# Stick-breaking attention with the keys on the partitions and its running sums on TensorE

## What is computed

```python
z = einsum('bqhd,bkhd->bhqk', qi, k) * scale            # scale = 0.125
strict = kpos[None, :] < qpos[:, None]
log_beta = log_sigmoid(z)
log_one_minus = where(strict, log_sigmoid(-z), 0.0)
after = lax.cumsum(log_one_minus, axis=3, reverse=True) - log_one_minus
weights = exp(where(strict, log_beta + after, -inf))
out = einsum('bhqk,bkhd->bqhd', weights, v)
```

## Time and profile before

| | us |
|---|---|
| median of 3 runs | 4967.44 (4967.3 to 4972.65) |
| the profiled execution | 4978.45 |
| its span in the trace | 4976.6 |
| stick stage of the first such block, 3214.2 to 3371.2 | 157.0 |
| stick stage of the second, 4313.2 to 4471.9 | 158.7 |

### The profile page before, as it was taken

The page is one execution under the profiler, slowest core; times in us unless marked ns, Lnnn a source line. Parts: engine busy times, 40 slices in busy tenths (PEclk is TensorE's granted clock), DMA queues, the critical chain, the costliest instruction groups (busy, mean ns, idle before and its releaser), DMA issues. The chain is left out here.

```text
span 4976.6 us, 90377 instructions
## 1 busy us (share of the span) xinstructions
PE 4460.7 (90%) x38676; PEld 3119.2 (63%) x38676; DVE 2113.1 (42%) x3803; ACT 1495.0 (30%) x2632; POOL 792.0 (16%) x499
## 2 busy tenths in 40 slices
PE   6899899988998899979999798978999988878999
PEld 3566666666555554465443776757788866656787
DVE  2555554554355552131111446354443446345343
ACT  2343333332222221010000334453232334443232
POOL 0021111110132230000000221243000321333000
PEclk9899999988999999989999899989999999999999
DMA  6200000000110123427999311214222211214221
GB/s 228 71 28 11 17 19 17 5 24 16 43 43 29 48 87 131 154 107 302 405 403 411 122 63 50 69 49 168 88 98 77 94 56 48 69 61 154 98 102 51
DMA packets 86824, 512.05 MB, mean 103 GB/s; under 512 B 10504, under 2 KB 11032, under 8 KB 45848
## 3 DMA queue, kind: packets, MB, share of 16 engines
q1 hardware_dynamic: 86424, 506.28, 26.9%
HBM read 476.85 MB, written 29.38 MB: 102 GB/s over the span
## 5 line engine op out<-in xcount | busy, mean ns | idle before, releaser
L229 PE MATMUL ps<-rounded,rounded 128*128 128x512 f32 (+2 forms) x7968 | 1660.4, 367 | 44.3 <-DVE rounded L240 23.7
L229 PEld LDWEIGHTS ps<-rounded,rounded 128*128 128x128 f32 x7968 | 1338.1, 193 | 302.8 <-issue 36.1
L229 PE MATMUL ps<-lower 128*128 128x512 f32 (+10 forms) x4976 | 1075.0, 393 | 56.3 <-issue 22.8
L229 PE MATMUL ps<-upper 64*64 64x64 f32 (+8 forms) x15584 | 834.2, 259 | 152.0 <-DVE upper L268 38.2
L291 ACT ACTIVATE upper<-ps 128x512 f32<-128x512 f32 (+6 forms) x953 | 440.2, 491 | 1671.0 <-PE ps L229 1230.6
L229 PEld LDWEIGHTS ps<-upper 64*64 64x64 f32 (+4 forms) x15584 | 595.7, 145 | 419.8 <-issue 190.6
L229 PEld LDWEIGHTS ps<-lower 128*128 128x128 f32 (+3 forms) x4976 | 576.7, 184 | 442.9 <-issue 376.6
L229 PE MATMUL ps<-lower,upper 64*64 64x64 f32 (+6 forms) x7248 | 607.6, 305 | 47.5 <-DMA lower<-in_ada 20.3
L2620 POOL TENSOR_TENSOR rounded<-lower,rounded 128x1024 fp32r<-128x1024 f32 (+2 forms) x90 | 273.1, 3035 | 1952.3 <-ACT rounded L291 1952.0
L291 ACT ACTIVATE upper<-upper 128x512 f32<-128x512 f32 (+9 forms) x693 | 341.1, 500 | 584.1 <-DVE upper L248 131.4
L229 PEld LDWEIGHTS ps<-lower,upper 64*64 64x64 f32 (+3 forms) x7248 | 334.6, 143 | 258.7 <-issue 198.8
(11 more groups left out here) (91 smaller groups left out, 2351.0 us busy)
## 6 DMA issues: line engine op xcount, KB each, us to landing
lower<-in_ew SPq DMA_DIRECT2D x140, 1024.0 KB, 10.4
upper<-in_ew SPq DMA_DIRECT2D x52, 1024.0 KB, 13.1
lower<-in_b0f SPq DMA_DIRECT2D x16, 2048.0 KB, 7.4
lower<-in_b1f SPq DMA_DIRECT2D x16, 2048.0 KB, 7.7
upper<-in_ada SPq DMA_DIRECT2D x18, 1024.0 KB, 5.3
lower<-in_wrkv SPq DMA_DIRECT2D x8, 1728.0 KB, 7.3
lower<-in_b0g SPq DMA_DIRECT2D x24, 512.0 KB, 3.8
gad<-upper SPq DMA_DIRECT2D x48, 256.0 KB, 3.8
```

Source lines behind the costliest of these rows:

```text
L229: return self.e.matmul(out, lhsT, rhs, start=start, stop=stop)
```

## The change

The scores are computed transposed, with the keys on the partitions: for head `hh` and key block `j`, `ck` is the stationary side and the queries 128*j to 511 are the moving side. A head's lower triangle of blocks takes 1280 columns of PSUM in place of four units. The mask of the diagonal blocks is added by a matmul of the identity with a 128 x 128 mask (fp32r). The scale of 0.125 moves into the copy of the queries (`c0`). The running sum over keys, which was a scan of VectorE along the free side, becomes matmuls along the partitions, with a triangle of -1 and a full square of -1 as weights, on two fp32r parts (`lost` and `rest`) of the losses; they are written over the scores in the same PSUM banks, and VectorE adds the copy of the scores (`chance`) to them. The weights then already have the form that the value matmuls want, and the transposes and their copies go. Every elementwise step handles a whole head (128 x 1280). Two heads are in flight, each with three PSUM banks of its own (`take_at`).

The order of the stage is written out: scores of head `hh`; sums of head `hh-1`; `early` filler items; values of head `hh-1`; `late` filler items. The remainders of the weights (`part`) that stand behind `meet B` are computed by VectorE. The diff, cut to its core:

```diff
-    p2 = {"mla": add(k <= q), "sb": add(k < q), "g2": add((k <= q) & ((q - k) % 4 == 0)),
+    p2 = {"mla": add(k <= q), "sb": add(i[:, None] < i[None]), "tri": -f(i[:, None] >= i[None]), "one": -f(up | True), "g2": add((k <= q) & ((q - k) % 4 == 0)),
...
-    b.on = RC[:, 2048:2560]
-    b.trip = [RA[:, 1536 * z:1536 * z + 1536] for z in range(6)]
+    at = ROUNDED + 4096
+    b.soft = [k.plain(at + 3840 * z, 1280) for z in range(2)]
+    b.chance = [k.plain(47272 + 1280 * z, 1280) for z in range(2)]
+    b.lost = [k.rounded(at + 3840 * z + 1280, 1280) for z in range(2)]
+    b.raw = [k.plain(at + 3840 * z + 2560, 1280) for z in range(2)]
+    b.rest = [k.rounded(at + 3840 * z + 2560, 1280) for z in range(2)]
+    b.sums = k.rounded(43176, 512)
...
+    end = b.order.index(("meet", "B"))
+    for key in (step[1] for step in b.order[end:] if step[0] == "part"):
+        b.units[key].late = True
...
+def part_done(k, l, key):
+    return k.parts.dve if k.b2[l].units[key].late else k.parts.pool
+
+
+def part_vector(k, v, l, key):
+    u = k.b2[l].units[key]
+    if u.late:
+        v.wait_ge(k.parts.act, "high", l, key)
+        v.tt(k.parts.dve, u.low, u.raw, u.high.bitcast(F32), SUB, "low", l, key)
+
+
 def part_gpsimd(k, g, l, key):
     u = k.b2[l].units[key]
+    if u.late:
+        return
...
-    drain([lane("stick", 32, 5, z) for z in range(6)], filler, 1.4)
+    for hh, (early, late) in enumerate(((2, 2), *[(3, 3)] * 6, (3, 2), (3, 0))):
+        if hh < 8:
+            out.append(("stick", hh, 0))
+        if hh:
+            out.append(("stick", hh - 1, 1))
+        out += itertools.islice(filler, early)
+        if hh:
+            out.append(("stick", hh - 1, 2))
+        out += itertools.islice(filler, late)
...
+BLOCK_AT = (0, 512, 1024, 896)
+
+
+def block_cut(j, i=None):
+
+    at = BLOCK_AT[j] + 128 * ((i or j) - j)
+    return slice(at, BLOCK_AT[j] + 512 - 128 * j)
...
-            pe.wait_ge(k.parts.pool, "low", l, key)
+            pe.wait_ge(part_done(k, l, key), "low", l, key)
...
+    def stick(hh, s):
+        team, slot, use = k.lane[hh % 2], hh % 2, ("stick", l, hh)
+        e = slice(64 * slot, 64 * slot + 64)
+        if s == 0:
+            ps = banks.take_at(use, 3 * slot, 3)
+            pe.wait_ge(M.act, "sums", l)
+            for j in (0, 1, 3, 2):
+                pe.mm(ps[:, block_cut(j)], b.ck[e, hh // 2, 128 * j:128 * j + 128], b.cq[e, hh // 2, 128 * j:512], j != 3, False)
+                last = pe.mm(ps[:, BLOCK_AT[j]:BLOCK_AT[j] + 128], b.sums[:, 256:384], b.sums[:, 384:512], False, j != 1)
+            last.then_inc(team.pe.up("score", l, hh), 1)
+            return
+        ps = k.pair(use)
+        if s == 1:
+            pe.wait_ge(team.dve, "parts", l, hh)
+            pe.wait_ge(team.act, "kept", l, hh)
+            for j in (3, 2, 1, 0):
+                for i in range(j, 4):
+                    for part in (b.lost[slot], b.rest[slot]):
+                        last = pe.mm(ps[:, block_cut(j, i)], b.sums[:, 128:256] if i > j else b.sums[:, 0:128],
+                                     part[:, block_cut(i)], j != 1 and i == j and part is b.lost[slot],
+                                     j != 3 and i == 3 and part is b.rest[slot])
+            last.then_inc(team.pe.up("less", l, hh), 1)
+        else:
+            pe.wait_ge(team.act, "exp", l, hh)
+            for i in range(4):
+                for j in range(i + 1):
+                    p = b.chance[slot][:, BLOCK_AT[j] + 128 * (i - j):BLOCK_AT[j] + 128 * (i - j) + 128]
+                    for half in (slice(0, 64), slice(64, 128)):
+                        last = pe.mm(ps[half, 1280 + 64 * i:1344 + 64 * i], p[:, half], b.cv[:, j, 64 * hh:64 * hh + 64],
+                                     j == 0, j == i)
+            last.then_inc(team.pe.up("value", l, hh), 1)
+            banks.give(use, team.dve, "value", l, hh)
...
-            v.copy(P.dve, dst, v3(ps, 256)[:, :, 0:tok_width(t)] if name == "tok" else ps, *use)
+            if t == "c0":
+                v.ts(P.dve, dst, ps, 0.125, MUL, event=use)
+            else:
+                v.copy(P.dve, dst, v3(ps, 256)[:, :, 0:tok_width(t)] if name == "tok" else ps, *use)
...
-    def stick(u, s):
-        o = Unit(k, l, "stick", u)
-        t, nk = o.lane.dve, o.nk
-        z, a_, r = (o.buf[:, 512 * q:512 * q + nk] for q in range(3))
-        if s == 1:
-            v.wait_ge(o.lane.pe, "score", *o.u)
-            v.stt(t, z, k.pair(("score", *o.u))[:, 0:nk], 0.125, o.mask, MUL, ADD, "score", *o.u)
-        elif s == 2:
-            v.wait_ge(o.lane.act, "log", *o.u)
-            v.stt(t, a_, z, 0.0, a_, MAX, ADD)
-            v.wait_ge(t)
-            v.e.tensor_tensor_scan(r[:, ::-1], b.on[:, 0:nk], a_[:, ::-1], 0.0, MUL, ADD).then_inc(t.up("sum", *o.u), 1)
-        elif s == 3 and o.i % 2:
-            v.wait_ge(o.lane.pe, "turn", *o.u)
-            v.copy(t, z, k.pair(("turn", *o.u))[:, 0:nk], "turn", *o.u)
-        elif s == 4:
-            v.wait_ge(o.lane.pe, "value", *o.u)
-            v.copy(t, o.out, k.pair(("value", *o.u))[:, 0:64], "value", *o.u)
+    def stick(hh, s):
+        team, slot = k.lane[hh % 2], hh % 2
+        t, ps = team.dve, k.pair(("stick", l, hh))
+        if s == 0:
+            v.wait_ge(team.act, "log", l, hh)
+            v.stt(t, b.raw[slot], ps[:, 0:1280], 0.0, b.soft[slot], MAX, ADD, "loss", l, hh)
+            v.wait_ge(team.act, "lost", l, hh)
+            v.tt(t, b.rest[slot], b.raw[slot], b.lost[slot].bitcast(F32), SUB, "parts", l, hh)
+        elif s == 1:
+            v.wait_ge(team.pe, "less", l, hh)
+            v.tt(t, b.chance[slot], b.chance[slot], ps[:, 0:1280], ADD, "less", l, hh)
+        else:
+            v.wait_ge(team.pe, "value", l, hh)
+            v.copy(t, b.otC[:, :, 64 * hh:64 * hh + 64], v3(ps[:, 1280:1536], 64), "value", l, hh)
...
-    def stick(u, s):
-        o = Unit(k, l, "stick", u)
-        nk, t = o.nk, o.lane.act
-        z, a_ = o.buf[:, 0:nk], o.buf[:, 512:512 + nk]
-        if s == 1:
-            a.wait_ge(o.lane.dve, "score", *o.u)
-            a.act(t, a_, z, AF.Abs)
-            a.act(t, a_, a_, AF.Exp, scale=-1.0)
-            a.act(t, a_, a_, AF.Ln, "log", *o.u, bias=1.0)
-        elif s == 2:
-            a.wait_ge(o.lane.pool, "less", *o.u)
-            a.act(t, z, z, AF.Exp, "exp", *o.u)
-        elif s == 3 and o.i % 2 == 0:
-            a.wait_ge(o.lane.pe, "turn", *o.u)
-            a.copy(t, z, k.pair(("turn", *o.u))[:, 0:nk], "turn", *o.u)
+    def stick(hh, s):
+        team, slot = k.lane[hh % 2], hh % 2
+        t, ps, p = team.act, k.pair(("stick", l, hh)), b.soft[slot]
+        if s == 0:
+            if hh == 0:
+                a.copy(M.act, b.sums[:, 0:128], c2["tri"])
+                a.copy(M.act, b.sums[:, 128:256], c2["one"])
+                a.copy(M.act, b.sums[:, 256:384], k.c["ident"])
+                a.copy(M.act, b.sums[:, 384:512], c2["sb"], "sums", l)
+            a.wait_ge(team.pe, "score", l, hh)
+            a.act(t, p, ps[:, 0:1280], AF.Abs)
+            a.copy(t, b.chance[slot], ps[:, 0:1280], "kept", l, hh)
+            a.act(t, p, p, AF.Exp, scale=-1.0)
+            a.act(t, p, p, AF.Ln, "log", l, hh, bias=1.0)
+            a.wait_ge(team.dve, "loss", l, hh)
+            a.copy(t, b.lost[slot], b.raw[slot], "lost", l, hh)
+        elif s == 1:
+            a.wait_ge(team.dve, "less", l, hh)
+            a.act(t, b.chance[slot], b.chance[slot], AF.Exp, "exp", l, hh)
...
-        elif name == "stick":
-            u, s = z
-            o = Unit(k, l, name, u)
-            if z == [0, 0]:
-                g.wait_ge(M.pool)
-                g.e.memset(b.on, 1.0).then_inc(M.pool.up("ones", l), 1)
-            if s == 2:
-                y, r = o.buf[:, 0:o.nk], o.buf[:, 1024:1024 + o.nk]
-                g.wait_ge(o.lane.dve, "sum", *o.u)
-                g.wait_ge(o.lane.pool)
-                g.e.tensor_tensor(y, y, r, SUB).then_inc(o.lane.pool.up("less", *o.u), 1)
```

More of the change, by code:

```diff
@@ L1 @@
+import itertools
 import numpy as np
@@ L311, in take, with take_at @@
         self.i = i + n if i + n < self.hi else self.lo
+        for b in range(i, i + n):
+            assert self.free.get(b, ()) is not None, "no bank is free"
+            if self.free.get(b):
+                self.pe.wait_ge(*self.free[b])
+            self.free[b] = None
+        self.pe.k.bank[use] = (i, n)
+        return self.pe.k.ps[:, 512 * i:512 * (i + n)]
+    def take_at(self, use, i, n):
         for b in range(i, i + n):
@@ L2573, in block2_units @@
         u = Bag()
-        u.key, u.n, u.piece = key, n, piece
+        u.key, u.n, u.piece, u.late = key, n, piece, False
         if j < FIRST_UNITS:
@@ L2764, in __init__ @@
         hh, i = 2 * (u // 8) + u % 2, u // 2 % 4
-        if name == "stick":
-            hh, i = 2 * (u // 2 % 4) + u % 2, 3 - u // 8
         e = slice(64 * (hh % 2), 64 * (hh % 2) + 64)
@@ L2785, in __init__ @@
             self.den = b.rd[:, self.q:self.q + 1]
-        else:
```

(33 more changed lines are left out.)

## The result

The changed kernel is slower: 5056.91 us in the median of 4 runs (5054.29 to 5063.88) against 4967.37 (4 runs) of the kernel before, a ratio of 1.0177, interval 1.0165 to 1.0190. That is +89.5 us where +73 was predicted (5040), inside the range. The two profiled executions differ by less, 5053.0 - 4976.6 = +76.4 us of span; the one of before lay 11 us above its median, the one of after (5054.76) at its own.

The account below looks back on a forecast made before the run. TensorE's work plus its waits was taken as the bound: 122.5 us work, 52 waits, 3 ends and 17 clock made a 194.5 us stage, +73 us for both, median 5040 us, range 4988 to 5072.

Parts of the forecast that it names:

- gate steps, 47: TensorE's gate work in the stick stage: 0.231 us a record, 1.39 a step of six, 65.2 us in all, unchanged.
- sums, a head: TensorE's 20 fp32r matmuls of 128 to 512 columns for one head's running sums: 2.8 us.
- The chain and its place: From the end of hh's scores to the values of hh-1: 12.9 us, hh-1's add and Exp queued behind hh's front.
- The scores: One head's scores on TensorE: 1280 columns of plain fp32 at the unpaired price, 2.15 us, with four masks 2.6.
- The values: One head's value matmuls on TensorE: 40 records, priced from 32 in 1.40 us, so 1.76 us.
- The waits: TensorE's waits in one stick stage: 41 us in iterations 2 to 7, 4.6 and 6.1 around head 0, 52 in all.
- The clock: Half speed behind eight TensorE waits of 4.6 us and more, 2.2 us each: 17 us a stage, ends 0 and 22.
- The signs: Expected trace: stage near 194 us, seven waits of 6 to 7.3 us ahead of values, some 22 us score to score.
- The contended price: VectorE's chain instructions 40% longer if contending with GpSimd, stage 13 us longer; expected not to apply, 1280 columns at 1.48 us.
- Parts on VectorE: Eleven parts at 1.22 us on VectorE, 13.5 us in the filler's slots, counted as nothing; 25 us if cover fails.
- Rival (a): The fill covers the chain in the stick stages: stage 128 us, -60 us for both, 4907 us; chance 11%.
- "The late filler does not help": Late filler in the stick stage stands behind the values, so it was said not to help against TensorE's waits.

Follow-up runs that it names:

- the mended order: The changed kernel with only its list reordered, the Exp of head hh-1 ahead of Exp and Ln of hh: 1.0020 of the kernel before, 4976.68 us.

## Why the prediction was right, point by point

Its result and its mechanism hold: 5040 was predicted for the median and 5056.91 measured, inside 4988 to 5072, and the longest waits are ahead of the values, for the Exp. That the stage came out within 3 us (194.5 against 197.4) is in part luck, since three terms are off by 8 us or more and two of them cancel the third. The terms for the first stage, predicted against measured:

| term | predicted | measured |
|---|---|---|
| gate steps, 47 | 65.2 | 66 (0.235 a record: 60 in 14.13 us behind the attention) |
| scores, a head | 2.6 | 3.87 (3248.05 to 3251.92) |
| sums, a head | 2.8 | 3.0 (5.78 with two gate steps of 1.39) |
| values, a head, full clock | 1.76 | 1.40 |
| scores' end to the values | 12.9 | 12.4 |
| waits ahead of sums and values | 52 | 37.9 |
| start and end of the stage | 3 | 2.4 |
| cost of the clock | 17 | about 25, what is left of 197.4 (27.5 by slices) |
| stage | 194.5 | 197.4 |

- **The chain and its place** (12.9 us, the Exp of hh-1 behind the front of hh): right within 0.5 us, and shown by the mended order.
- **The scores**: the mis-sized term. "With four masks it is 2.6" took the masks at the price of fp32r matmuls in a row; the changes between 64 and 128 rows (eight a head, four of them upward) cost 1.3 us more a head, 10 us a stage. A pair of 64-row heads could not show it, as no 128-row matmul stood inside.
- **The values**: 1.76 came from 32 records in 1.40 us. They stood in part in the stretch at half clock; at full clock 40 take 1.40.
- **The waits**: 37.9 in place of 52. About 4 of the 14 us are the shorter chain and the longer sums. The greater part is work that runs at 1.2 GHz and so covers more. In iteration 1 the scores of head 0 and the two gate steps behind them take 9.8 us (3214.30 to 3224.07, clock 0.65) where 5.4 were counted, and the waits there are 1.5 and 3.9 in place of 4.6 and 6.1. In three of the six middle iterations the sums run slowly behind the scores: the iteration above has its 32 records of sums and filler in 7.33 us and waits 5.09; the one of head 2's scores (from 3251.92) has its 32 in 5.78 and waits 6.64. So two errors, of the clock and of the waits, are one and cancel in part.
- **The clock**: I put all of its falls behind waits. Some stand behind the scores, which need no wait.
- **The signs**: seven waits of 6 to 7.3 us were named; there are six of 5.1 to 6.6 and one of 3.9. From scores to scores it is 22 to 25 us, "some 22" was named.
- **The contended price**: 40% came from a mean of 0.952 us. The trace has six of those eight instructions at 0.67 to 0.69 us and two at 1.68 and 1.86, so what was read as a longer price was a hold in two cases, each beside a GpSimd instruction. That the 1280-wide instructions take 1.48 us with GpSimd quiet was right (1.49).
- **Parts on VectorE** at nothing: right here. It is not so in the kernel before, where the same edit costs 22 us.
- **Rival (a)**, that the fill covers the chain, did not come true. Its deciding point was the right one: in the five runs in which the Exp is early the stages are 134 to 161 us. I had the far end at 128.
- **"The late filler does not help"**: nearly. Without it the copy of the values is exposed, 9.3 us a stage.
- Of +89.5 us in the medians the two profiled executions account for 76.4. The other 13 come from which execution was profiled: that of before lay 11 us above its median, that of after 2 below. Runs of the kernel before lie between 4952 and 4982 us over all comparisons; what makes them differ stays open.

## What to carry to other kernels

When work is pipelined over two items on engines that execute in order, write down for each engine which item's instruction stands ahead of which: a short tail of the old item queued behind a long front of the new one costs the whole front, and no amount of idle time on that engine shows it in the busy shares. Filler covers only what comes before the wait in the same queue; count it in gate steps, not in list items. And look at the order of the list before judging an algorithm: the same instructions were 1.8% slower than the old ones in one order and, with the masks grouped and the filler dealt out anew, 0.8% faster in another. Last, a term that comes out right in total can hide two that are wrong: compare waits, busy time and clock one by one.

## What the runs showed of the hardware

- A 128-row matmul behind a 64-row one waits until that is through: 0.52 us behind 512 columns (1.05 against 0.53 from the first score to its mask), and 1.1 us a head for its four such changes (3.87 against 2.74). fp32 and fp32r in turn show no price of their own (2.55 us with both over 128 rows, 2.6 had been worked out without one).
- The granted clock fell to 1.2 GHz behind a stretch in which the profile has TensorE busy for all of 8.8 us, when 3.9 us of it were matmuls with such changes in between (0.54 in the 3.4 us behind). In the same place without the changes it stayed at 2.4 GHz, but two falls in 64-row scores were left, next to waits of 0.7 to 1.5 us, and none with 128-row scores. Before I had seen falls only behind waits.
- A VectorE instruction with two SBUF inputs that started 0.33 us behind a GpSimd weight remainder ran until 0.4 us behind its end: 2.65 us in place of 0.53 for 384 columns. The 1280-wide ones were never met in this way.
- The 20 fp32r matmuls of the sums, eight of them of 128 columns, took 3.0 us (5.78 less two gate steps) where 2.8 had been worked out with the 0.113 us of 160 columns. Only the total was timed; with the other widths at what was counted for them it leaves about 0.14 for each of the eight, so 128 columns were no cheaper than 160.
